# A fused two-block network on one core: modulation rows of tiles 4 to 11 formed by GpSimd instead of TensorE

## The chip, the cores and the metric

The kernel runs on one core of a Trainium2 chip (trn2). The metric is the device time of one launch in microseconds (us). Three timed runs of the kernel before gave 2313.67 us as the median, with 2313.07 and 2315.28 as the ends.

## What is computed

The input is `x`, 256 tokens of 1024 numbers, and a conditioning vector `c` of 1024. The first block begins with a modulation vector that scales, shifts and gates the later steps:

```python
mod = jax.nn.silu(c) @ w_ada[l] + b_ada[l]          # w_ada: 1024 x 6144
shift_m, scale_m, gate_m, shift_f, scale_f, gate_f = jnp.split(mod, 6, axis=-1)
h = rmsnorm(x, g_pre_mix[l]) * (1.0 + scale_m) + shift_m
...                                                 # projection, retention, dilated attention
x = x + gate_m * rmsnorm(mixed, g_post_mix[l])
h = rmsnorm(x, g_pre_ffn[l]) * (1.0 + scale_f) + shift_f
moe = expert_choice_moe(h, w_router[l], w_gate_e[l], w_up_e[l], w_down_e[l])
x = x + gate_f * rmsnorm(moe, g_post_ffn[l])
```

`mod` has 6144 numbers, which the kernel makes in twelve tiles of 512 columns. Tiles 0 to 3 give `shift_m` and `scale_m`, which the first projection needs. Tiles 4 to 11 give `gate_m`, `shift_f`, `scale_f` and `gate_f`, which are needed only after the output projection of the mixer. Sixteen experts follow, and then two layers of a second block.

## The kernel before, in words

All is in float32, and the large products of the mixer are split into a high and a low part, with three matmuls in place of one. Each engine has its own program (`@block.sync` for the loads, `gpsimd`, `tensor`, `scalar`, `vector`), and they meet only at semaphores. The order inside each program is written out by hand.

**Loads.** SyncE issues all loads in one order, `first_tiles()` (line 101): the first four modulation tiles, win 3, win 4, ada 4, ada 5, win 5, win 0, ada 6, win 1, ada 7, win 2, ada 8, wout 0, ada 9, wout 1, ada 10, ada 11, and then the tiles of the experts ("ada" is a tile of `w_ada`, "win" of the input projection, "wout" of the output projection; each has 2 MB, 4096 floats in each partition). Even ada tiles from 4 on lie in ring slot 2, odd ones in slot 3; the others alternate between slots 0 and 1. A load waits until the tile before it in its slot is used (`load`, line 571, waits for `tile_done`), and what stands behind it in the queue waits with it. So the load of ada 7 waits for the release of ada 5 and stands behind that of win 1, which waits for the release of win 5.

**A modulation tile from 4 on.** TensorE's `modulation(i)` (line 790) waits for the tile and makes eight products with `silu_c` as stationary operand, 32 equal columns of it, in four groups of 32 rows of one PSUM bank (bank 7 for all of tiles 4 to 11); each product is two matmul instructions. It then releases the slot. VectorE's `modulation(i)` (line 1840) copies the bank to `modrow[i % 2]`, 128 partitions x 512. TensorE's `modulation_columns(i)` (line 803) makes four columns of it, with `first_rows`, which is 1 in four partitions and 0 elsewhere, as the vector that sums the four groups. VectorE's `modulation_columns(i)` (line 1850) adds the bias and writes four columns of `mod`. In TensorE's list the calls stand between the units of the input projection, attention, retention and the output projection (lines 969 to 1070), in VectorE's list between its own steps (lines 1999 to 2074).

**Around it.** A projection tile goes through ScalarE (`split_first`, line 1418, casts the high part) and VectorE (`split_first`, line 1865, subtracts the high part from the raw tile in two halves of 128 x 2048, line 1869) before TensorE's `win_unit` or `wout_products` uses it. Between the tiles VectorE also makes the constants of the later layers (`layer_constants`, line 1920: seventeen instructions of 28 or 20 elements, each of which waits for the one before it), the decay arguments (lines 1943 to 1945) and the attention sums (line 1976). TensorE's last work before the normalisation of the mixer's output is `wout_products` with the first four blocks of the mixer's output (lines 1064 to 1068), behind `modulation_columns(11)`.

**GpSimd** writes constants at the start (lines 716 to 731) and then has nothing until the layers of the second block (lines 735 to 749).

## Time and profile before

| | |
|---|---|
| median of three runs | 2313.67 us |
| span of the profiled execution | 2312.3 us (the profile states no other time for it; the median is 1.4 us above the span) |
| TensorE matmul busy | 2014.7 us, 87% |
| VectorE busy | 1018.0 us, 44% |
| ScalarE busy | 727.7 us, 31% |
| GpSimd busy | 28.3 us, 1%, 23 instructions |
| DMA | 657.03 MB, mean 284 GB/s |

Times in the trace count from the start of the span. The mixer of the first block runs from about 42 to 182 us, normalisation and routing to about 228 us, the sixteen experts to about 1150 us, and the rest is the second block. "Busy" leaves out the time in which an engine waits or issues; "idle before" is the wait ahead of an instruction with what ended it.

### The profile page before, as it was taken

What the parts mean: (1) busy time and instruction counts of PE and PEld (TensorE: products, weight loads), DVE (VectorE), ACT (ScalarE), POOL (GpSimd) and SP (SyncE); (2) the same over time, 40 slices, a digit from 0 to 9 for tenths busy, and PEclk for the clock granted to TensorE, in tenths of its full rate; (3) what the DMA queues carried; (4) which work ended last, traced back from release to release, by engine and by line L of the source; (5) the groups of instructions that cost most, each with busy time, mean ns of one, the idle gap of its engine ahead of it and who ended that gap; (6) DMA issues with size and microseconds to landing.
All of it is one profiled execution on the core that took longest, in us unless ns stands there. A gap on an engine that the chain in (4) does not pass through costs nothing.

```text
span 2312.3 us, 30721 instructions
## 1 busy us (share of the span) xinstructions
PE 2014.7 (87%) x12679; PEld 1488.8 (64%) x12680; DVE 1018.0 (44%) x1136; ACT 727.7 (31%) x799; POOL 28.3 (1%) x23
## 2 busy tenths in 40 slices
PE   7997877777777777776699999999999999999999
PEld 6886333333333333333378899998888889998888
DVE  5653000000000000000277786877777767777776
ACT  3542000000000000000144446554444444745443
POOL 0000000000000000000000002000000000200000
PEclk9996978788887778887899999999999999999999
DMA  8784999999999999999935665455565566545554
GB/s 318 250 333 177 382 430 427 430 427 430 427 429 427 430 427 430 427 430 427 403 136 171 163 207 178 159 198 191 149 210 182 160 186 210 183 151 196 183 161 131
DMA packets 233161, 657.03 MB, mean 284 GB/s; under 512 B 6948, under 2 KB 121956, under 8 KB 208484
## 3 DMA queue, kind: packets, MB, share of 16 engines
q1 hardware_dynamic: 233060, 655.62, 74.1%
q8 instruction: 71, 1.16, 0.2%
q14 instruction: 30, 0.25, 0.0%
HBM read 654.54 MB, written 1.05 MB: 284 GB/s over the span
## 4 chain that ended last, share of the span: by engine, by line
issue 85%; PE 13%; DVE 1%; POOL 1%; ACT 0%; DVEq 0%; POOLq 0%; ACTq 0%
PE psum L1219 3%; PE psum L1220 2%; PE psum L1241 2%; PE psum L1242 2%; PE psum L1243 2%; PE psum L1320 2%; PE psum L1321 1%; DVE ring_r L2151 1%; PE psum L1287 0%; POOL work L742 0%; ACT ring_r L1624 0%; PE psum L1288 0%; POOL work L741 0%; POOL work L743 0%; DVE x L2447 0%
## 5 line engine op out<-in xcount | busy, mean ns | idle before, releaser
L2151 DVE TENSOR_TENSOR ring_r<-ring,ring_r 128x2048 fp32r<-128x2048 f32 (+2 forms) x182 | 452.7, 2518 | 100.7 <-ACT ring_r L1624 100.0
L1624 ACT CAST ring_r<-ring 128x2048 fp32r<-128x2048 f32 (+2 forms) x180 | 360.1, 2041 | 289.4 <-PE psum L1321 121.7
L1219 PE MATMUL psum<-work_r,ring_r 128*128 128x512 f32 x1280 | 446.3, 394 | 3.3 <-DVE ring_r L2151 3.3
L1220 PE MATMUL psum<-work_r,ring_r 128*128 128x256 f32 x1280 | 357.7, 279 | 0.0
L1219 PEld LDWEIGHTS psum<-work_r,ring_r 128*128 128x128 f32 x1280 | 239.8, 187 | 59.1 <-issue 3.9
L1136 PE MATMUL psum<-ring,work 128*32 128x512 f32 x1280 | 185.2, 716 | 101.2 <-DMA ring<-in_w_up_e_dram 101.2
L1241 PE MATMUL psum<-work_r,ring_r 128*128 128x256 f32 x928 | 263.7, 284 | 2.5 <-DVE ring_r L2151 2.5
L1242 PE MATMUL psum<-work_r,ring_r 128*128 128x256 f32 x928 | 262.4, 283 | 0.0
L1243 PE MATMUL psum<-work_r,ring_r 128*128 128x256 f32 x928 | 262.0, 282 | 0.0
L1320 PE MATMUL psum<-work_r,ring_r 128*128 128x512 f32 x704 | 247.9, 397 | 3.2 <-DVE ring_r L2151 3.2
L1220 PEld LDWEIGHTS psum<-work_r,ring_r 128*128 128x128 f32 x1280 | 241.5, 189 | 0.0
L2140 DVE COPY work<-psum 128x256 f32<-128x256 f32 x16 | 6.8, 425 | 464.8 <-PE psum L1117 464.8
L1321 PE MATMUL psum<-work_r,ring_r 128*128 128x256 f32 x704 | 197.5, 280 | 0.0
L1136 PEld LDWEIGHTS psum<-ring,work 128*32 128x32 f32 x1280 | 39.8, 121 | 237.6 <-DMA ring<-in_w_up_e_dram 154.7
L2145 DVE TENSOR_TENSOR work<-work,psum 128x512 f32<-128x512 f32 x16 | 11.0, 687 | 410.2 <-PE psum L1136 410.2
L1241 PEld LDWEIGHTS psum<-work_r,ring_r 128*128 128x128 f32 x928 | 177.2, 191 | 5.2 <-issue 4.0
L1242 PEld LDWEIGHTS psum<-work_r,ring_r 128*128 128x128 f32 x928 | 177.3, 191 | 0.1
L1243 PEld LDWEIGHTS psum<-work_r,ring_r 128*128 128x128 f32 x928 | 177.1, 191 | 0.0
L1320 PEld LDWEIGHTS psum<-work_r,ring_r 128*128 128x128 f32 x704 | 132.1, 188 | 36.0 <-issue 4.3
L2226 DVE TENSOR_REDUCE work<-psum 128x512 f32<-128x1024 f32 x88 | 107.3, 1221 | 75.5 <-PE psum L1220 68.7
L1158 PE MATMUL psum<-work 128*32 128x512 f32 x512 | 84.6, 794 | 55.9 <-DMA work<-in_w_down_e_dram 55.9
L1321 PEld LDWEIGHTS psum<-work_r,ring_r 128*128 128x128 f32 x704 | 133.0, 189 | 0.0
(301 smaller groups left out, 2388.4 us busy)
## 6 DMA issues: line engine op xcount, KB each, us to landing
ring<-in_w_up_e_dram SPq DMA_DIRECT2D x48, 2048.0 KB, 28.6
ring<-in_ffn_w_up_dram SPq DMA_DIRECT2D x41, 2048.0 KB, 8.0
work<-in_w_gate_e_dram SPq DMA_DIRECT2D x32, 2048.0 KB, 11.6
ring<-in_w_gate_e_dram SPq DMA_DIRECT2D x32, 2048.0 KB, 14.2
ring<-in_w_down_e_dram SPq DMA_DIRECT2D x32, 2048.0 KB, 36.6
work<-in_w_down_e_dram SPq DMA_DIRECT2D x32, 2048.0 KB, 30.3
ring<-in_w_in_dram SPq DMA_DIRECT2D x25, 2048.0 KB, 8.2
ring<-in_ffn_w_down_dram SPq DMA_DIRECT2D x32, 1408.0 KB, 7.0
```

What stands on the lines that cost most here:

```text
L1136: mm = pe.matmul(dst[32 * g:32 * g + 32, :], xe[:, 2 * q + k, :], w[:, k, 512 * g:512 * (g + 1)], start=(q == 0 and k == 0), stop=(q == FB ...
L1158: mm = pe.matmul(two_banks[1][32 * b:32 * b + 32, 512 * half:512 * (half + 1)], hiddenT[:, b, 32 * q:32 * q + 32], w[:, b, 512 * half:512 ...
L1219: pe.matmul(dst, w_hi[:, k, cols], h_both(k), start=(k == 0), stop=False)
L1220: mm = pe.matmul(dst[:, 0:S], w_lo[:, k, cols], h_hi_[:, S * k:S * (k + 1)], start=False, stop=(k == KD - 1))
L1241: pe.matmul(out_b, w_hi[:, k, cols], hi[:, tokens], start=(k == 0), stop=False)
L1242: pe.matmul(out_b, w_hi[:, k, cols], lo[:, tokens], start=False, stop=False)
L1243: mm = pe.matmul(out_b, w_lo[:, k, cols], hi[:, tokens], start=False, stop=(k == n_k - 1))
L1320: pe.matmul(dst, w_hi[:, k, :], u_both(k), start=(k == 0), stop=False)
L1321: mm = pe.matmul(dst[:, 0:S], w_lo[:, k, :], u_hi[:, S * k:S * (k + 1)], start=False, stop=(k == FK - 1))
L1624: act.copy(hi_unit(name, unit), raw_unit(name, unit)).then_inc(hi_ready, 1)
L2151: dve.tensor_tensor(lo_unit(name, unit), raw_unit(name, unit), hi_unit(name, unit).bitcast(F32), ALU.subtract).then_inc(lo_ready, 1)
L2226: dve.tensor_reduce(dst.rearrange("p (c t) -> p c t", c=2), src, AX.X, ALU.add).then_inc(emptied["dve"], 1)
```

## The change

GpSimd makes the rows of tiles 4 to 11. It waits for the tile, multiplies each of its eight blocks of 512 in place by its column of `silu_c` (one number in each partition), and adds the blocks as a tree: 2048 elements, then 1024, then 512 from the last two blocks into `modrow[i % 2]`. After each of the three steps and after the eighth product it waits for its own completion. The last addition waits for TensorE's columns of tile i - 2; only behind it are the slot released and the row announced. TensorE sums over all 128 partitions with a vector of ones, and its wait for VectorE's addition of the tile before (`mod_ready`) moves from the products to the columns. TensorE's products and VectorE's copies of tiles 4 to 11 go. Tiles 0 to 3 and the order of the loads stay.

```diff
@@ constants, GpSimd
             pool.memset(mean_d[:], 1.0 / D)
+            pool.memset(ones_col[:], 1.0)
@@ GpSimd, behind its constants
+            def modulation(i):
+                name = ("ada", i)
+                s = ring_plan.slot(name)
+                w = slot_view(name, KD, 512)
+                halves = w.rearrange("p k (b n) -> p k b n", b=2)
+                pool.wait_ge(loaded[s], ring_plan.loaded(name))
+                for k in range(KD):
+                    scaled = pool.tensor_scalar(w[:, k], w[:, k], silu_c[:, k, 0:1], None, ALU.mult)
+                step(scaled)
+                step(pool.tensor_tensor(w[:, 0:4], w[:, 0:4], w[:, 4:8], ALU.add))
+                step(pool.tensor_tensor(w[:, 0:2], w[:, 0:2], w[:, 2:4], ALU.add))
+                pool.wait_ge(modT_done, max(4, i - 1))
+                step(pool.tensor_tensor(modrow[i % 2], halves[:, 0], halves[:, 1], ALU.add))
+                pool.sem_inc(tile_done[s], 1)
+                pool.sem_inc(modrow_ready, 1)
+
+            pool.wait_ge(silu_c_ready, 1)
+            for i in range(4, 12):
+                modulation(i)
@@ TensorE
-            def modulation(i):
-                rows = mod_bank(i)
-                pe.wait_ge(mod_ready, i)
-                name = ("ada", i)
-                pe.wait_ge(loaded[ring_plan.slot(name)], ring_plan.loaded(name))
-                w = slot_view(name, KD, 512)
-                for k in range(KD):
-                    g = k % 4
-                    mm = pe.matmul(rows[32 * g:32 * g + 32, :], silu_c[:, k, :], w[:, k, :],
-                                   start=(k < 4), stop=(k >= KD - 4), skip_group_check=True)
-                mm.then_inc(tile_done[ring_plan.slot(name)], 1)
...
                     pe.wait_ge(modrow_ready, i if i >= 4 else {1: 1, 0: 2, 3: 3}[i])
+                if i >= 4:
+                    pe.wait_ge(mod_ready, i)
                 for c in range(4):
                     mm = pe.matmul(mod_bank(i)[:, c:c + 1], modrow[i % 2][:, c // 2, P * (c % 2):P * (c % 2 + 1)],
-                                   first_rows[:], start=True, stop=True)
+                                   (first_rows if i < 4 else ones_col)[:], start=True, stop=True)
@@ the lists of TensorE and of VectorE, eight places in each
-            modulation(4)
...
-            modulation(11)
```

## Rows read from the trace of the kernel before

**Rows 1.** Busy time in stretches: engine busy (instructions), PEclk, DMA share, GB/s

```profile
60.00:70.00 10.00, 10.00 (x85) 8.39 (x85) 3.87 (x7) 4.88 (x4) 0.00 (x0) 1.00 0.32 96
...
170.00:180.00 10.00, 10.00 (x86) 10.00 (x85) 0.44 (x4) 1.09 (x2) 0.00 (x0) 1.00 0.98 407
...
200.00:210.00 10.00, 9.62 (x45) 9.35 (x46) 3.38 (x13) 6.95 (x16) 0.00 (x0) 0.50 0.00 0
```

**Rows 2.** Groups of TensorE, 55 to 182 us: busy, mean ns, idle before

```profile
L799 PE MATMUL psum<-ring,work 128*32 128x512 f32 x128 | 15.4, 598 | 0.0
```

**Rows 3.** Timeline of TensorE: start us, us, line

```profile
60.91 1.92 PE L799 MATMUL psum<-ring,work 128*32 128x512 f32 x16
62.77 0.39 PE L904 MATMUL psum<-work_r,ring_r 128*128 128x256 f32 x1
...
72.42 0.50 PE L894 MATMUL psum<-ring_r,work_r 128*128 128x512 f32 x1
...
168.88 0.95 PE L810 MATMUL psum<-first_rows,pool_u 128*128 128x1 f32 x8
...
181.16 0.28 PE L1044 MATMUL psum<-work_r,ring_r 128*128 128x256 f32 x1
```

**Rows 4.** Timeline of GpSimd, 1398 to 1417 us

```profile
1398.86 2.00 POOL L741 TENSOR_TENSOR work<-pool_u 128x1084 f32<-128x1084 f32 x1 [1395.84 <-DVE pool_u L2214]
1400.93 3.46 POOL L742 TENSOR_TENSOR work<-work 128x807 f32<-128x807 f32 x1
1404.47 1.07 POOL L743 TENSOR_TENSOR work<-work 128x530 f32<-128x530 f32 x1
...
1410.96 5.74 POOL L749 TENSOR_TENSOR work<-work 128x2560 f32<-128x2560 f32 x1 [4.59 <-ACT work L1738]
```

**Rows 5.** Timeline of VectorE over the same stretch

```profile
1400.09 2.92 DVE L2151 TENSOR_TENSOR ring_r<-ring,ring_r 128x2048 fp32r<-128x2048 f32 x1 [1.31 <-ACT ring_r L1624]
...
1408.41 2.28 DVE L2151 TENSOR_TENSOR ring_r<-ring,ring_r 128x2048 fp32r<-128x2048 f32 x1
...
1411.21 9.84 DVE L2151 TENSOR_TENSOR ring_r<-ring,ring_r 128x2048 fp32r<-128x2048 f32 x2
```

**Rows 6.** Timeline of GpSimd at the start

```profile
1.19 0.29 POOL L717 TENSOR_SCALAR_AFFINE_SELECT ident<-ident 128x128 f32<-128x128 f32 x1 [0.24 <-POOL ident L716]
...
1.61 0.56 POOL L722 IOTA work<- 128x512 f32 x1
```

**Rows 7.** Groups of VectorE, 45 to 170 us: busy, mean ns, idle before

```profile
L1869 DVE TENSOR_TENSOR ring_r<-ring,ring_r 128x2048 fp32r<-128x2048 f32 x14 | 31.9, 2285 | 4.0 <-ACT ring_r L1425 3.9
L1976 DVE CUSTOM_DVE_ANT_0 work<-work 128x256 f32<-128x256 f32 x16 | 6.1, 419 | 0.0
L1848 DVE COPY pool_u<-psum 128x512 f32<-128x512 f32 x8 | 5.5, 690 | 12.4 <-PE psum L799 12.4
...
L1945 DVE TENSOR_TENSOR work<-work 128x512 f32<-128x512 f32 x4 | 2.8, 694 | 0.1
...
L1894 DVE TENSOR_TENSOR ring_r<-ring,ring_r 128x512 fp32r<-128x512 f32 x3 | 2.1, 685 | 0.0
L1944 DVE TENSOR_SCALAR work<-work,soft 128x512 f32<-128x512 f32 x4 | 1.9, 486 | 0.1
...
L1928 DVE SCALAR_TENSOR_TENSOR soft<-soft 128x28 f32<-128x28 f32 x8 | 1.5, 188 | 0.3
```

**Rows 8.** Timeline of SyncE's queue, 34 to 86 us: issues of loads

```profile
34.11 2.14 SPq L580 DMA_DIRECT2D ring<-in_w_ada_dram  x2
...
84.57 0.37 SPq L580 DMA_DIRECT2D ring<-in_w_in_dram  x1
84.98 0.58 SPq L580 DMA_DIRECT2D ring<-in_w_ada_dram  x1
```

**Rows 9.** Issues, KB and us to landing: tile 4's, then tile 7's

```profile
ring<-in_w_ada_dram SPq DMA_DIRECT2D x1, 2048.0 KB, 11.8
...
ring<-in_w_ada_dram SPq DMA_DIRECT2D x1, 2048.0 KB, 13.2
```

**Rows 10.** Timeline of TensorE, one matmul early and one late in the first projection

```profile
42.46 0.41 PE L871 MATMUL psum<-work_r,ring_r 128*128 128x256 f32 x1
...
48.37 0.28 PE L871 MATMUL psum<-work_r,ring_r 128*128 128x256 f32 x1
```

More of the change, by code:

```diff
@@ L318, in block_kernel @@
         mean_d = sb("mean_d", [P, 1])
+        ones_col = sb("ones_col", [P, 1])
         std = sb("std", [P, 8])
@@ L975, in _ @@
             att_scores(0)
-            modulation(5)
             win_unit(4)
@@ L981, in _ @@
             att_transpose(0)
-            modulation(6)
             win_unit(6)
@@ L993, in _ @@
             att_transpose(3)
-            modulation(7)
             win_unit(10)
@@ L1000, in _ @@
             att_transpose(5)
-            modulation(8)
             ret_scores(0)
@@ L1007, in _ @@
             ret_values(0)
-            modulation(9)
             ret_values(1)
@@ L1014, in _ @@
             att_values(3)
-            modulation(10)
             pe.wait_ge(att_done, ATT_HEADS // 2)
@@ L2000, in _ @@
             layer_constants()
-            modulation(4)
             split_first(("win", 5), (0,))
@@ L2006, in _ @@
             decay_log(0)
-            modulation(5)
             att_sums(0)
@@ L2016, in _ @@
             split_first(("win", 0), (1,))
-            modulation(6)
             decay_log(1)
@@ L2029, in _ @@
             split_first(("win", 2), (1,))
-            modulation(7)
             att_scores(6)
@@ L2039, in _ @@
             att_scores(7)
-            modulation(8)
             ret_decay(0)
@@ L2046, in _ @@
             ret_decay(2)
-            modulation(9)
             ret_decay(3)
@@ L2051, in _ @@
             split_first(("wout", 1), (1,))
-            modulation(10)
             mixin_low_att(1)
@@ L2072, in _ @@
                                   ALU.subtract).then_inc(mixin_lo_ready, 1)
-            modulation(11)
             modulation_columns(11)
```

## The prediction, made before the changed kernel was run

> **What bounds the kernel now.** I began with the busy time in stretches. Up to about 182 us TensorE is busy in the whole of every stretch, at a granted clock of 1.00, which is 2.4 GHz [rows 1]; so the mixer lasts as long as TensorE's list. At 200 us the DMA share is 0.00 [rows 1]: the first nine expert tiles are in, and nothing is loaded until the experts start at about 228 us. So whatever moves TensorE's end of the mixer, 181.4 us (the last matmul of wout starts at 181.16 [rows 3]), moves the experts and the end of the kernel by as much, and later loads cost nothing while those tiles still land before the experts start.
>
> Then the groups of the engines that the change touches. The products to be removed are 128 matmuls, 15.4 us busy with no wait ahead of them [rows 2]. The timeline shows what one tile takes of TensorE's list: from 60.91 to 62.77, 1.86 us [rows 3]; eight take 14.9 us. VectorE's copies take 5.5 us, most of the wait ahead of them being for these products [rows 7].
>
> Last the only places where GpSimd does arithmetic, in the second block, laid beside VectorE [rows 4, 5]. VectorE's subtraction of 128 x 2048, both inputs in SBUF, takes 2.28 us when GpSimd rests. Two of them issued at 1411.21 took 9.84, although they need 4.5: GpSimd had begun 2560 elements at 1410.96 and held them until 1416.70, and 1416.70 + 4.5 is about 1421.05. At 1400.09 a third took 2.92: it got going when GpSimd's 1084 elements ended at 1400.86. GpSimd's next instruction then took 3.46 for 807 elements, since VectorE held it until 1403.01. One excludes the other in both directions, and whoever waits goes next.
>
> **What is removed.** TensorE: 14.9 us of its list. VectorE: 5.5 us. Neither counts unless the columns are ready when TensorE comes to them.
>
> **What is added.** A column product against ones in place of the four-row vector has the same shape: nothing. The one memset is beside the start: nothing. What costs is GpSimd's tile, 11 instructions:
> - Additions: 2048 elements at the rate of the 2560 row (5.74) are 4.6 us; 1024 by the 1084 row (2.00) 1.9; 512 by the 530 row (1.07) 1.05 [rows 4]. Together 7.6. With the rate of the short rows for all of them it would be 3.7 + 1.9 + 0.95 = 6.5.
> - Products: no row shows a multiplication of 512 by a column. Below, the write-only iota of 512 takes 0.56 with its overhead, and a one-input select of 128 takes 0.29 [rows 6]; I take 0.43 as the lower end, the bare rate of the iota. Above, a two-input addition of 530 takes 1.07 [rows 4]. One input read and one output written is nearest to the iota: 0.6. Eight are 4.8 us.
> - So a tile is 12.4 us where TensorE needed 1.86, and eight are 99 us; their 24 waits for completion (0.07 between rows at 1404.39 and 1404.47 and the like) add 2.
>
> The Trainium skill, in "GPSIMD Engine Reference", section 3.1, gives 4497 ns for an addition of 2048 and 769 ns for a loop over 512. The first agrees with the 4.6 above; by the second the products would be 6.2 us a tile, and the end some 11 us later than mine.
>
> **The shared resource.** VectorE's instructions in this stretch that read two tensors in SBUF, or one at more than one element a cycle, are 31.9 + 6.1 + 2.8 + 2.1 us, twice 1.9 for the two kinds of scalar step ahead of line 1945, 1.5 + some 2.0 for the small ones of the constants, and about 1 for the rest [rows 7]; the scalar steps count because 0.49 us for 512 elements is under the 0.69 of the addition. About 51 us. Copies from PSUM and reductions don't count. Tile 4 lands at 34.11 + 11.8 = 45.9 [rows 8, 9]. GpSimd's last tile thus ends no earlier than 45.9 + 99 + 2 + 51 = 198 us.
>
> That this can't be beaten by order: TensorE's own wait for a VectorE result is longer too. From 46 us VectorE's steps alternate with GpSimd's. Ten or so of VectorE's until 54.6 take 7 us longer. Sixteen of the seventeen small constants each wait for one GpSimd instruction, 12.4/11 = 1.1 us on average: the chain that ended at 60.6 ends at about 81. Behind it in VectorE's list stands the subtraction of win 5, which then ends at about 86. TensorE, which began win 5 at 72.42 [rows 3], would be ready at 70.6 and waits until 86: 15 us. The release of win 5 at 84.57 goes to about 99, and with it, in SyncE's queue, the load of win 1 and behind it that of tile 7 (84.98 [rows 8]), which lands 13.2 later [rows 9], at 112. GpSimd, done with tile 6 at about 103, stands idle for 8 us, of which VectorE uses half. So 198 + 4 = 202 us for tile 11.
>
> Between 112 and 202 GpSimd goes from tile to tile in 17 to 19 us each, 12.4 of its own and 5 of VectorE's; TensorE waits for columns 10 until about 188, and then needs some 14 us to come to columns 11, at 202 too. Both ways give the same point.
>
> **The tail.** Columns 11 start at 168.88 now [rows 3] and at 202 then: 33 us later, the wout products behind them take as long. After the wait they start at the lower level of the clock: at 200 us, behind waits, the granted clock is 0.50, which is 1.2 GHz [rows 1], and a matmul early in the mixer takes 0.41 us against 0.28 for the same one later [rows 10]. I add 2 us for that, between nothing and the 4 that two cold starts would cost. The experts' loads into slots 2 and 3 wait for tiles 10 and 11, until 202; the six behind take 5.2 us each at 407 GB/s [rows 1] and are in at about 233, against a start of the experts at 263. Covered, as is the rest behind.
>
> **Sum.** 33 + 2 = 35 us on the profiled execution of 2312.3 us of span. The median stands 1.4 us above that span, and the same is added: 2312.3 + 1.4 + 35 = 2348.7, say 2348 us, 1.5% slower. A measurement of this kernel can tell about 0.2%, 4.6 us.
>
> The Trainium skill's rule that speaks against this change is in "SBUF — State Buffer", "Who interferes with whom": an exclusive lock for an instruction's whole length between GpSimd and VectorE's instructions with two SBUF inputs. Rows 4 and 5 agree, in both directions; without the lock the sum would be that of rival A.
>
> **Rivals.**
> - **A. No exclusion in this stretch** (not slower). GpSimd's tile is 12.6 us beside VectorE. The load of tile 10 stands behind that of wout 1, which waits for TensorE's last unit of win 2, now about 7 us earlier, at 124; tile 10 lands at about 140 and is ready at 152.5. TensorE comes to columns 10 at 152.4 now and gains nothing until there; it then saves the products of tile 11, 1.9 us, and a little more. 2311 us. It decides if VectorE's steps of 2.28 us stay 2.28. For it speaks only that the excluded operations in rows 5 are of one kind; against it both rows. 7%, of which 3% with cheap products as well, when it is over 4.6 us faster.
> - **B. Cheap GpSimd.** Products 0.43 and additions 6.5: 10 us a tile, 19 less in eight. 202 - 19 is 183, 15 us late, 16 to 17 with a little more idling. 2331 us. For it: the short rows at 1.9 ns an element [rows 4]. 20%.
> - **C. Dear products**, 1.07 as for two inputs [rows 4]: 30 us more over eight tiles, and about 3 more as VectorE's small steps wait longer and the load of tile 7 comes later: 2348 + 33 = 2381 us. A product of 0.8 gives some 14 us more than mine, 2362. 20% for anything above 2362.
> - **D. The small steps slip in** between GpSimd's instructions and don't wait: the chain of constants ends at 68, TensorE's 15 us go, but GpSimd's eight tiles stay, and 8 us less is all: 2340. It lies within the forecast.
>
> Forecast (with D) 53%, A 7%, B 20%, C 20%. The forecast's own range is 2336 to 2362. For 8 in 10 I leave out A, the lowest of B and the upper part of C: 2326 to 2380. Faster 0.03; same 0.04, the rest of A; slower 0.93. That GpSimd doesn't do the work is no case: TensorE's columns have no other source.
>
> **What would show it.** Right: VectorE's subtractions at line 1869 of 3 us and more on average in place of 2.28, the wait of TensorE for the first half of win 5 about 15 us, GpSimd busy or blocked almost without a gap from 46 to 202 us with 17 to 19 us a tile after tile 7, columns 11 at about 202, waits of TensorE for GpSimd at columns 10 and hardly at 4 to 7, and experts that take as long as before. Wrong: line 1869 at 2.28 (A); products of 0.45 or of 1 us (B, C); additions of 2048 at 3.7 us; TensorE's longest wait elsewhere than at win 5 and columns 10; or an expert stage that absorbs or adds time.

## The result, and the profile after

The changed kernel took 2386.97 us (median of four runs, 2385.57 to 2388.2); the kernel before, beside it, 2313.37 us (median of four, 2311.38 to 2315.28). The ratio is 1.0311, with a 95% interval of 1.0299 to 1.0323: 73.6 us slower. The forecast of 2348 us had the sign right and the size at less than half, and its range ended at 2380.

GpSimd's groups of the profile after, from 44 to 240 us (line, engine, operation, shapes, count | busy us, mean ns of one | idle time before and what ended it):

```profile
L745 POOL TENSOR_SCALAR ring<-ring,work 128x512 f32<-128x512 f32 x64 | 117.9, 1859 | 45.0 <-DMA ring<-in_w_ada_dram 43.0 <-POOL pool_u L750 2.0
L747 POOL TENSOR_TENSOR ring<-ring 128x2048 f32<-128x2048 f32 x8 | 37.6, 4701 | 0.7
L748 POOL TENSOR_TENSOR ring<-ring 128x1024 f32<-128x1024 f32 x8 | 20.9, 2613 | 0.6
L750 POOL TENSOR_TENSOR pool_u<-ring 128x512 f32<-128x512 f32 x8 | 12.3, 1533 | 0.6
```

The only wait for a load is the first, 43.0 us until tile 4 is in; behind it GpSimd works without a gap. Its timeline shows the first and the last tile; beside the last, VectorE had almost nothing to share:

```profile
46.04 15.97 POOL L745 TENSOR_SCALAR ring<-ring,work 128x512 f32<-128x512 f32 x8 [42.99 <-DMA ring<-in_w_ada_dram]
...
217.13 13.08 POOL L745 TENSOR_SCALAR ring<-ring,work 128x512 f32<-128x512 f32 x8 [0.29 <-POOL pool_u L750]
230.29 4.58 POOL L747 TENSOR_TENSOR ring<-ring 128x2048 f32<-128x2048 f32 x1
234.94 2.34 POOL L748 TENSOR_TENSOR ring<-ring 128x1024 f32<-128x1024 f32 x1
237.36 1.26 POOL L750 TENSOR_TENSOR pool_u<-ring 128x512 f32<-128x512 f32 x1
```

VectorE's only wide instructions beside it are four at 224.65 to 227.3, of which these two read two tensors in SBUF; one of the eight products, that of 226.37, took 2.30 us and the other seven 1.56:

```profile
226.02 1.29 DVE L2068 TENSOR_TENSOR work_r<-work,work_r 128x512 fp32r<-128x512 f32 x2
```

Eight products with none of that beside them take 12.35 us, as in experiment 8, so one begins every 1.54 us:

```profile
170.55 12.35 POOL L746 TENSOR_SCALAR ring<-ring,work 128x512 f32<-128x512 f32 x8 [0.29 <-POOL pool_u L751]
```

With additions of 4.49, 2.34 and 1.26 us and the steps between them a tile alone is 21.0 us, and eight are 168; the span from 46.04 to 238.62 is 192.6, so sharing with VectorE adds 25.

TensorE's waits, first in the view of waits (us in total, times, longest), then in its timeline, and the last matmul of the output projection:

```profile
PE psum L822 <- POOLq L752: 56.6, 6, 13.7
```

```profile
238.81 1.87 PE L822 MATMUL psum<-ones_col,pool_u 128*128 128x1 f32 x8 [5.57 <-POOLq L752]
...
253.73 0.28 PE L1049 MATMUL psum<-work_r,ring_r 128*128 128x256 f32 x1
```

Against [rows 3] the columns of tile 11 start 238.81 - 168.88 = 69.9 us later and the last matmul 253.73 - 181.16 = 72.6. That is the 73.6 us within 1 us. The experts behind take as long as before: VectorE's copies for the first and the last expert start 864.8 us apart (before 864.7):

```profile
L2136 DVE COPY work<-psum x16: 424/425/425, 300.4 to 1165.2; 128x256 f32<-128x256 f32 x16
```

VectorE's subtractions and attention sums, and in between the constants, from 45 to 240 us (compare [rows 7]: 2285 and 419 ns):

```profile
L1873 DVE TENSOR_TENSOR ring_r<-ring,ring_r 128x2048 fp32r<-128x2048 f32 x14 | 40.4, 2895 | 1.1 <-ACT ring_r L1429 1.1
L1980 DVE CUSTOM_DVE_ANT_0 work<-work 128x256 f32<-128x256 f32 x16 | 20.9, 1339 | 0.0
...
L1939 DVE TENSOR_SCALAR nsp<-soft 128x20 f32<-128x20 f32 x1 | 4.5, 4503 | 0.0
...
L1932 DVE SCALAR_TENSOR_TENSOR soft<-soft 128x28 f32<-128x28 f32 x8 | 2.4, 297 | 0.3
```

One instruction of 20 elements took 4.5 us: it came beside the addition of 2048. The eight at line 1932 came beside products and took 0.30 each on average, where the prediction had let each wait for 1.1. So there are two kinds of GpSimd work here, and the experiments take them apart.

### The profile page after: what moved, and what is told of

Its sections match the earlier page's. It is cut to its first block, busy times and chain, and to the rows that moved or that the text cites. A ratio compares the mean times of both kernels' runs of the same rounds, so it can differ in the third digit from the quotient of the medians.

```text
span 2385.1 us, 30565 instructions
## 1 busy us (share of the span) xinstructions
PE 2018.9 (85%) x12552; PEld 1502.0 (63%) x12552; DVE 1048.0 (44%) x1128; ACT 727.7 (31%) x799; POOL 216.9 (9%) x112
## 3 DMA queue, kind: packets, MB, share of 16 engines
HBM read 654.54 MB, written 1.05 MB: 275 GB/s over the span
## 4 chain that ended last, share of the span: by engine, by line
issue 76%; PE 13%; POOL 9%; DVE 1%; DMA 1%; SPq 0%; ACT 0%; DVEq 0%; POOLq 0%; ACTq 0%
POOL ring L745 5%; PE psum L1223 3%; PE psum L1224 2%; POOL ring L747 2%; PE psum L1245 2%; PE psum L1246 2%; PE psum L1247 2%; PE psum L1324 1%; POOL ring L748 1%; PE psum L1325 1%; DVE ring_r L2147 1%; POOL pool_u L750 1%; DMA ring<-in_w_ada_dram 0%; PE psum L1291 0%; SPq L599 0%
```

## The experiments

The theory at this point: GpSimd's pace sets the time, since it is busy without a gap and the last columns follow it; the products cost 1.5 to 1.6 us where I had 0.6; the additions keep VectorE out, the products hardly. The rivals: the time is made of VectorE's lateness; or of TensorE's lower clock behind its waits. The sum of TensorE's waits left room for the last: 56.6 us for GpSimd and 8.1 for VectorE, less 14.9 of removed products, is 50 and not 73.

**1. Prices alone.** The kernel before, with single GpSimd instructions put where GpSimd had been idle and VectorE waits.

```diff
+            pool.wait_ge(onehot_ready, 1)
+            for n in (128, 256, 512, 1024):
+                step(pool.tensor_scalar(scratch[:, 0:n], scratch[:, 0:n], col, None, ALU.mult))
+            for n in (128, 512, 1024):
+                step(pool.tensor_scalar(scratch[:, 0:n], scratch[:, 0:n], 0.5, None, ALU.mult))
+            for n in (128, 512):
+                step(pool.tensor_tensor(scratch[:, 0:n], scratch[:, 0:n], scratch[:, 512:512 + n], ALU.add))
+            for n in (128, 512, 1024):
+                step(pool.tensor_tensor(scratch[:, 0:n], scratch[:, 0:n], col.broadcast_to([P, n]), ALU.mult))
+            for n in (128, 512):
+                step(pool.tensor_copy(scratch[:, 0:n], scratch[:, 512:512 + n]))
```

> The kernel before, with GpSimd instructions on an unused buffer added at the start of the experts, where VectorE is nearly idle; each waits for the one before it. This prices the product by itself. In the changed kernel a product of 512 by a column takes 1.56 us and starts 1.63 after the one before. Theory P1, a fixed cost for the column operand: products of 128, 256, 512, 1024 take about 1.25, 1.35, 1.56, 2.0 us, and products by a constant 0.5 to 0.7 us at 512. Theory P2, a rate of 3 ns an element whatever the operand: 0.45, 0.8, 1.56, 3.1 us, and the same with a constant. Theory P3, contention with VectorE made up most of it: 0.6 us at 512 here. An addition of 512 should take 1.1 to 1.3 us, and a product of 512 by a column spread over the elements (two inputs) as much. The whole kernel: within 0.3% of before, since GpSimd has nothing else to do there.

The one run took 2311.56 us, the kernel before beside it 2314.81 (median): within the 0.3% that was expected. GpSimd's groups in it:

```profile
L740 POOL TENSOR_SCALAR pool_mix<-pool_mix,mean_d 128x1024 f32<-128x1024 f32 x1 | 2.8, 2842 | 0.1
L742 POOL TENSOR_SCALAR pool_mix<-pool_mix 128x1024 f32<-128x1024 f32 x1 | 2.8, 2769 | 0.1
L746 POOL TENSOR_TENSOR pool_mix<-pool_mix,mean_d 128x1024 f32<-128x1024 f32 x1 | 1.9, 1892 | 0.1
L740 POOL TENSOR_SCALAR pool_mix<-pool_mix,mean_d 128x512 f32<-128x512 f32 x1 | 1.6, 1564 | 0.1
...
L744 POOL TENSOR_TENSOR pool_mix<-pool_mix 128x512 f32<-128x512 f32 x1 | 1.3, 1270 | 0.1
L746 POOL TENSOR_TENSOR pool_mix<-pool_mix,mean_d 128x512 f32<-128x512 f32 x1 | 1.0, 1039 | 0.1
```

A product of 512 by a column takes 1.564 us with nobody beside it, and 2.842 at 1024: (2.842 - 1.564)/512 = 2.5 ns an element. A constant as factor costs nearly the same (2.769 at 1024), so most of it is the one-input form and not the reading of the column; that is P2 of the expectation, with a slope of 2.5 ns where it had 3. The same product written with two inputs, the second being the column spread over the row, takes 1.039 and 1.892: 1.67 ns an element. The one-input form is the dearer one, dearer even than the addition of two tensors.

**2. No products.** The eight products are left out, the additions stay.

```diff
-                for k in range(KD):
-                    scaled = pool.tensor_scalar(w[:, k], w[:, k], silu_c[:, k, 0:1], None, ALU.mult)
-                step(scaled)
```

> The changed kernel without the eight products of each tile (so tiles 4 to 11 are summed without their factors silu(c)); additions, waits and columns are unchanged. GpSimd's tile falls from 21.7 us alone to about 8.5. Theory A, the price of the products is what made the change 73 us slower, through GpSimd being late for TensorE: most of it goes, and the kernel is between 2307 us (no exclusion between VectorE and GpSimd: 6.6 us faster than before) and 2324 us (each of GpSimd's additions blocks VectorE and the other way round: 10 us slower). Theory B, the loss is mainly from waits on VectorE and the queues, whatever the products cost: more than 2340 us.

2337.94 us, ratio 1.0103 (1.0069 to 1.0138): 50 of the 73 us are gone, fewer than theory A had, and the time lies between the two theories' bands. GpSimd's and VectorE's groups:

```profile
L744 POOL TENSOR_TENSOR ring<-ring 128x2048 f32<-128x2048 f32 x8 | 43.2, 5404 | 91.4 <-DMA ring<-in_w_ada_dram 90.9 <-POOL pool_u L747 0.5
...
L1870 DVE TENSOR_TENSOR ring_r<-ring,ring_r 128x2048 fp32r<-128x2048 f32 x14 | 49.8, 3568 | 0.6 <-ACT ring_r L1426 0.6
L1977 DVE CUSTOM_DVE_ANT_0 work<-work 128x256 f32<-128x256 f32 x16 | 26.9, 1716 | 0.0
```

GpSimd now waits for loads (90.9 us) and TensorE never for GpSimd. What remains is VectorE: its subtractions take 3.57 us against 2.29, more than in the changed kernel, and TensorE's waits for VectorE and ScalarE add up to 24 us.

**3. No additions.**

```diff
-                step(pool.tensor_tensor(w[:, 0:4], w[:, 0:4], w[:, 4:8], ALU.add))
-                step(pool.tensor_tensor(w[:, 0:2], w[:, 0:2], w[:, 2:4], ALU.add))
                 pool.wait_ge(modT_done, max(4, i - 1))
-                step(pool.tensor_tensor(modrow[i % 2], halves[:, 0], halves[:, 1], ALU.add))
+                step(pool.tensor_copy(modrow[i % 2], halves[:, 0]))
```

> The changed kernel without GpSimd's additions: the eight products of a tile stay, and one copy of the first product's 512 columns goes into the modulation row in their place. It leaves out the sum over the other seven parts of the contraction in tiles 4 to 11. GpSimd takes 8 times 1.63 and about 0.6, so 13.7 us a tile. Theory A (the one-input products leave VectorE's two-input work alone; the exclusion comes from two-input instructions of GpSimd alone): VectorE's subtractions at L1873 fall from 2.90 us to their 2.3, its decay products at L1948 to under 0.8; eight tiles take 110 us, the last one is held by its load rather than by GpSimd and is done at 165 to 175, so that TensorE makes the columns of tile 11 at about the time of the kernel before (168.9); 2300 to 2316 us. Theory B (the products hold VectorE too, for a part of each): VectorE's subtractions stay at 2.6 us or more and the time is 2325 to 2345 us.

2331.53 us, ratio 1.0068 (1.0041 to 1.0095). GpSimd, VectorE, and the products' shortest, median and longest in ns:

```profile
L745 POOL TENSOR_SCALAR ring<-ring,work 128x512 f32<-128x512 f32 x64 | 119.9, 1891 | 51.8 <-DMA ring<-in_w_ada_dram 50.3 <-POOL pool_u L748 1.4
...
L1871 DVE TENSOR_TENSOR ring_r<-ring,ring_r 128x2048 fp32r<-128x2048 f32 x14 | 33.4, 2392 | 7.6 <-ACT ring_r L1427 7.5
L1978 DVE CUSTOM_DVE_ANT_0 work<-work 128x256 f32<-128x256 f32 x16 | 8.5, 569 | 0.0
```

```profile
L745 POOL TENSOR_SCALAR ring<-ring,work x64: 1557/1566/5838, 46.1 to 179.0; 128x512 f32<-128x512 f32 x64
```

58 of the 73 us are gone. VectorE's subtractions came as theory A had them, 2.39 us on average, 0.1 more than before; its time didn't, and 2331.53 lies in theory B's band. The products suffer: the median is 1.57 us, and one took 5.84, 4.27 more; VectorE's timeline has two subtractions back to back in that tile:

```profile
47.58 4.48 DVE L1871 TENSOR_TENSOR ring_r<-ring,ring_r 128x2048 fp32r<-128x2048 f32 x2
```

So VectorE's two-input work holds the products up. Whether a product holds VectorE depends on when the two meet. Here are two places of this run, each with a product, the subtraction that began beside it, and the next product:

```profile
65.28 1.57 POOL L745 TENSOR_SCALAR ring<-ring,work 128x512 f32<-128x512 f32 x1
66.38 2.29 DVE L1871 TENSOR_TENSOR ring_r<-ring,ring_r 128x2048 fp32r<-128x2048 f32 x1 [3.40 <-ACT ring_r L1427]
66.83 3.28 POOL L745 TENSOR_SCALAR ring<-ring,work 128x512 f32<-128x512 f32 x1
...
141.98 1.56 POOL L745 TENSOR_SCALAR ring<-ring,work 128x512 f32<-128x512 f32 x1
142.10 2.71 DVE L1871 TENSOR_TENSOR ring_r<-ring,ring_r 128x2048 fp32r<-128x2048 f32 x1
143.52 2.72 POOL L745 TENSOR_SCALAR ring<-ring,work 128x512 f32<-128x512 f32 x1
```

A subtraction that began 1.10 us behind the product's start took its 2.29, one that began 0.12 behind it took 0.43 more, and one at 0.34 behind (155.24, the product at 154.90) took 2.49, 0.2 more. All three fit a product that keeps VectorE out until 0.55 us after its start and has no use for the shared access after that: the products of 65.28 and 141.98 took no longer than alone, 1.57 and 1.56. That is B's mechanism, a part of each product, at 0.1 us on average where B had 0.3 or more. A product that comes to its start while VectorE has the access waits until VectorE is done, and these waits are the loss here: I had worked with 13.7 us a tile without them; products of 1.89 on average, and 7 us more of waits for loads than in the changed kernel, put the last row at 181.2 us and the last matmul at 195.6, 14.4 late.

**4. The products as one two-input instruction.**

```diff
-                for k in range(KD):
-                    scaled = pool.tensor_scalar(w[:, k], w[:, k], silu_c[:, k, 0:1], None, ALU.mult)
-                step(scaled)
+                step(pool.tensor_tensor(w, w, silu_c[:, :, 0:1].broadcast_to([P, KD, 512]), ALU.mult))
```

> The changed kernel with the eight products of a tile as one instruction: the whole tile of 4096 columns times the factors, each spread over its 512 columns (two inputs, in place). By the run with prices alone a two-input product took 1.892 us for 1024 columns (1.67 ns a column), so 4096 take about 7 us where eight one-input products take eight times 1.63, 13.1. A tile is then 7.0 + 4.5 + 2.35 + 1.26 = 15.1 us alone, not 21.7. Theory A (GpSimd's pace from 46 us to the last tile sets the time, and TensorE's columns of tile 11 follow it): eight tiles take 121 us and 20 to 35 of sharing with VectorE, or are held by their loads; the last ends at 187 to 205, TensorE makes the columns of tile 11 then, 18 to 36 us after its time in the kernel before; 2313 + 21 to 40, so 2334 to 2353 us, ratio 1.009 to 1.017. Theory B (the two-input product keeps VectorE's two-input instructions out for its whole 7 us, so that the gain of a cheaper product is paid back as waits on VectorE): GpSimd ends as early but TensorE's waits move to VectorE, 2355 to 2375 us. Theory C (the products' number or price is not what makes the change slow): 2380 us or more.

2383.47 us, ratio 1.0296 (1.0275 to 1.0318): nearly as slow as the change. It is beyond theory B's band and lies in theory C's, but the trace shows B's mechanism, larger than B had priced it. GpSimd's timeline (one product early, one later with its addition), then VectorE's over the later ones:

```profile
65.61 7.04 POOL L744 TENSOR_TENSOR ring<-ring,work 128x4096 f32<-128x4096 f32 x1 [0.26 <-POOL pool_u L748]
...
117.27 7.16 POOL L744 TENSOR_TENSOR ring<-ring,work 128x4096 f32<-128x4096 f32 x1 [13.29 <-DMA ring<-in_w_ada_dram]
124.50 4.57 POOL L745 TENSOR_TENSOR ring<-ring 128x2048 f32<-128x2048 f32 x1
```

```profile
117.56 7.15 DVE L1946 TENSOR_SCALAR work<-work,soft 128x512 f32<-128x512 f32 x1
124.74 4.87 DVE L1947 TENSOR_TENSOR work<-work 128x512 f32<-128x512 f32 x1
```

The price came as computed, 7.04 us in place of 12.35. But two steps of VectorE of 0.49 and 0.69 us alone [rows 7] took 7.15 and 4.87, from just after GpSimd's start to 0.3 and 0.5 us after the end of its instruction. TensorE waited up to 12.8 us for VectorE, the slots came free late, and GpSimd itself waited 78.8 us for loads. The same arithmetic, 43% cheaper, gained 3 us of 73, within the spread of its two runs (2379.14 and 2387.81): it had become the kind that excludes for its whole length.

**5. GpSimd's work beside the kernel before**, on scratch data of its own; nobody waits for it. Sixty-four products of 512, and three additions of 1024 and one of 512 for each tile.

```diff
+            for i in range(4, 12):
+                for k in range(KD):
+                    part = scratch[:, 512 * (k % 2):512 * (k % 2 + 1)]
+                    scaled = pool.tensor_scalar(part, part, mean_d[:, 0:1], None, ALU.mult)
...
+                for _ in range(2):
+                    step(pool.tensor_tensor(scratch, scratch, scratch, ALU.add))
+                step(pool.tensor_tensor(scratch, scratch, scratch, ALU.add))
+                step(pool.tensor_tensor(scratch[:, 0:512], scratch[:, 0:512], scratch[:, 512:1024], ALU.add))
```

> The kernel before, in which GpSimd beside it does the same instructions as in the change (eight products of 512, additions adding up to 2048, 1024 and 512 for each of eight tiles, one after the other from the landing of tile 4), but on a buffer that nobody reads; TensorE makes the rows as before and nobody waits for GpSimd. It shows contention alone. Theory C, contention for the shared SBUF access costs little of the 73 us and being late for columns the most: under 12 us slower, VectorE's 2048-wide subtractions 2.9 us on average instead of 2.28. Theory D, each product keeps VectorE out for all of its 1.56 us, so that VectorE's chains bound the mixer: over 40 us slower.

2320.12 us, ratio 1.0024 (1.0011 to 1.0038). VectorE's subtractions took 2.82 us and its sums 1.09, about as in the changed kernel, and this cost 5 us, which is theory C. So VectorE's lateness at this density is mostly hidden under TensorE's own work.

**6. One tile fewer.** Tile 4 stays on TensorE as before, GpSimd forms tiles 5 to 11.

```diff
-            for i in range(4, 12):
+            for i in range(5, 12):
                 modulation(i)
...
+            modulation(4)
             win_unit(3)
             modulation_columns(4)
```

> The changed kernel with tile 4 formed by TensorE as in the kernel before (1.9 us of it), tiles 5 to 11 by GpSimd. Theory A (GpSimd's unbroken work from 46 us to the last tile sets the time): tile 5 has landed by then, so each tile is ready one tile's time, 23.5 us, earlier, unless a load holds it; columns of tile 11 at 215 to 222; TensorE, which has 14 us of work between the columns of tiles 10 and 11, still waits for each; 2362 to 2371 us, ratio 1.021 to 1.025. Theory B (the time is made of TensorE's waits of VectorE and of its clock as much as of GpSimd's pace): 2374 to 2383 us.

2372.74 us, ratio 1.0246 (1.0219 to 1.0273), 14 us faster than the change and between the two bands. GpSimd began tile 5 at 52.10, not at 46, and waited 4.7 us for tile 6 (in all 53.8 us for loads, 10.8 more than with eight tiles); so it came to the last row at 224.07, 14.5 us earlier and not 23.5. The columns and the end moved by the same 14.5 and 14:

```profile
224.26 1.01 PE L835 MATMUL psum<-ones_col,pool_u 128*128 128x1 f32 x4 [6.01 <-POOLq L752]
```

The end follows GpSimd's last row one for one; that is theory A, with loads that I had not placed.

**7. The waits filled.** Matmuls of the identity ahead of five of the columns keep TensorE busy while it waits.

```diff
+WARM_AHEAD = {5: 45, 8: 35, 9: 55, 10: 52, 11: 22}
...
+                if i in WARM_AHEAD:
+                    pe.wait_ge(mod_ready, i)
+                    for _ in range(WARM_AHEAD[i]):
+                        pe.matmul(mod_bank(i)[:, 0:P], ident[:], ident[:], start=True, stop=True)
```

> The changed kernel with matmuls of the identity (results unused) put into five waits of TensorE for GpSimd's rows, ahead of the columns of tiles 5, 8, 9, 10 and 11: 45, 35, 55, 52 and 22 of them, about 0.21 us each at the full clock, so that each wait is nearly full and the granted clock does not fall after it. Theory A (GpSimd's pace alone sets the columns of tile 11 at 238.8 us; what TensorE loses to the lower clock ahead of that is taken out of its next wait): only the stretch behind the columns of tile 11 gains, where the last matmul of the output projection came 14.9 us after them and in the kernel before 12.3; 1 to 3 us less than the changed kernel's 2387, so 2384 to 2386. Theory B (the lower clock costs some 20 of the 73 us, as the sum of TensorE's waits, 56.6 us for GpSimd and 8.1 for VectorE less 14.9 of work removed, leaves open): 2365 to 2372 us. If the filled waits overrun, the time is above 2387 by the overrun.

2390.1 us (2388.02 to 2396.88), ratio 1.0335 (1.0318 to 1.0352): 4 us above theory A's band; it can't be told from the change, whose interval (1.0299 to 1.0323) it overlaps. Busy time in two stretches, the changed kernel's first and then this one's (PE busy, PEld, DVE, ACT, POOL, PEclk, DMA share, GB/s):

```profile
160.00:200.00 40.00, 16.85 (x72) 12.32 (x72) 18.34 (x16) 10.49 (x12) 38.94 (x19) 0.66 0.39 138
200.00:240.00 40.00, 21.15 (x146) 20.49 (x142) 6.76 (x14) 4.25 (x7) 37.85 (x20) 0.76 0.46 179
```

```profile
160.00:200.00 40.00, 31.39 (x227) 27.16 (x225) 9.76 (x10) 9.19 (x10) 38.94 (x19) 0.91 0.30 104
200.00:240.00 40.00, 35.39 (x288) 35.01 (x287) 6.46 (x16) 2.27 (x4) 36.68 (x19) 0.94 0.43 168
```

The granted clock rose from 0.66 to 0.91 and from 0.76 to 0.94, and nothing came of it: the columns of tile 11 started at 237.63 and the last matmul at 251.5, 2 us earlier in the trace, and the median isn't lower; where those 2 us went isn't settled. Theory B, 20 us for the clock, is out. A chain that waits for GpSimd again and again gives back in the next wait what it wins at the clock; the sum of the waits comes out short because the work between them took longer.

**8. Only the last two tiles.** From the kernel before: tiles 10 and 11 on GpSimd, their columns behind the output projection, where TensorE waits for the normalisation anyway.

```diff
+            for i in range(10, 12):
+                modulation(i)
...
-            modulation(10)
...
-            modulation(11)
...
             spread_columns(rstd_ready, 2, bank[5], TT, rstd_spread)
+            modulation_columns(10)
             square_sums(sq_ready, 9, 5, ms_done)
             spread_columns(rstd_ready, 3, bank[5], TT, rstd_spread)
+            modulation_columns(11)
```

> GpSimd makes the rows of tiles 10 and 11 only, which give gate_f and are not needed before the end of the experts; TensorE's columns of both move into its waits during the two normalisations at 187 and 199 us, and VectorE's additions with them. TensorE's list gets shorter by 3.7 us of products and by 1.7 us of columns. Tile 10 lands at 146 and is ready at about 170, tile 11 at about 193, before TensorE comes to the columns. Theory A (lateness is the cost, GpSimd's work is free where there is room): 3 to 5 us faster than before, 2308 to 2310. Theory D (VectorE is blocked by products): no gain or slower, since VectorE's split of wout 1 and the steps behind it fall into the same time. A third way: the expert loads into slots 2 and 3 wait for GpSimd, at 170 and 193 in place of 149 and 166, and the experts start late: 0 to 10 us slower.

2315.23 us, ratio 1.0002 (0.9988 to 1.0017). GpSimd's timeline with the additions of tile 11, and VectorE's eight additions to the stream in the view of their line (shortest, median and longest in ns):

```profile
182.98 4.49 POOL L748 TENSOR_TENSOR ring<-ring 128x2048 f32<-128x2048 f32 x1
187.55 2.40 POOL L749 TENSOR_TENSOR ring<-ring 128x1024 f32<-128x1024 f32 x1
```

```profile
L2112 DVE SCALAR_TENSOR_TENSOR x<-work,gains,x x8: 472/482/4761, 183.0 to 194.4; 128x256 f32<-128x256 f32 x8
```

One addition of 0.48 us took 4.76, the length of GpSimd's. TensorE's wait there became 8.2 us, where the kernel before has 3.4, and ate what the removed products had won.

**9. The last two with the two-input product.** The diff of experiment 4 on top.

> As in the run with only tiles 10 and 11 on GpSimd, but each with one two-input product of 4096 columns. There tile 11 was done at 191.3 and its additions of 183.0 to 190 kept VectorE's additions to the stream out, for which ScalarE and then TensorE waited 8.2 us; that took the 3 to 4 us that TensorE had gained. A tile is now 15 to 16 us alone, not 21.7: tile 10 from 147 to about 163, tile 11 to about 179, before VectorE's additions begin at 182. Theory A: the wait of 8.2 us shrinks to the kernel before's 3 to 5, and the kernel is 3 to 5 us faster than before: 2308 to 2311 us, ratio 0.998 to 0.9988. Theory B (the product of 7 us, now with two inputs, keeps VectorE's work at 147 to 155 and 163 to 170 out, which is on TensorE's path there): 2314 to 2322 us.

2321.11 us, ratio 1.0029 (1.002 to 1.0039): slower, theory B. The wait of 8.2 us did shrink, to 1.9. But TensorE waited 4.9 us at 151.6 and 5.6 us at 159.4 for VectorE, inside the stretch of the product and the additions.

**10. Only tile 10.** As experiment 8, with tile 11 on TensorE.

> Only tile 10 on GpSimd, with the change's eight products and three additions; tile 11 by TensorE as in the kernel before, and both tiles' columns behind the output projection. TensorE loses 1.86 us of work for tile 10. Tile 10 is formed from 147 to about 170, under the value products and the first part of the output projection, and nobody waits for GpSimd before the columns at 182. Theory A (a tile off TensorE is worth its 1.9 us where no wait takes it back): 2311 to 2312 us, ratio 0.999 to 0.9995. Theory B (VectorE's constants are late by the two additions of 4.5 and 2.4 us between 160 and 170): 2314 to 2318 us.

2313.26 us, ratio 0.9997 (0.9988 to 1.0006). The median lies between the two theories' bands. The first expert's copy came at 224.7 us against 227.8, 3.1 us earlier, and the last at 1089.4 against 1092.5; the medians differ by 0.9. The two kernels can't be told apart, and where the rest went isn't settled.

**11. Tile 11's additions held back.** As experiment 8, but they wait until VectorE has made its eight, and the columns come behind the router.

```diff
                 step(scaled)
+                if i == 11:
+                    pool.wait_ge(x_ready, 4 + KD)
                 step(pool.tensor_tensor(w[:, 0:4], w[:, 0:4], w[:, 4:8], ALU.add))
...
             tokens_out(0)
+            modulation_columns(11)
```

> Only tiles 10 and 11 on GpSimd, as in the first such run, but tile 11's additions wait until VectorE has made the stream's eight additions (at about 194 us), and TensorE makes the columns of tile 11 after the router and the first tokens, in a wait of its own. Theory A (the additions at 183 to 190 alone took the gain of that run back): TensorE's wait for the stream falls from 8.2 us to 2 to 4, the experts start 3 to 4 us earlier than in the kernel before, 2309 to 2312 us, ratio 0.998 to 0.999. Theory B (what is gained ahead of the experts is given back behind them, as the run with tile 10 alone hints: its first expert came 3.1 us earlier and its time fell by 0.9): 2312 to 2316 us. Theory C (the additions, now at 195 to 204, hold VectorE's products for the router, or the ring slot comes free too late for an expert's weights): 2316 us or more.

> The same kernel as the run with tile 11's additions held back, timed again on its own account: there its ratio was 0.9986 with an interval of 0.9972 to 1.0, which just touches no change. Theory A (additions placed beside no two-input work of VectorE let the removed TensorE work come through): 0.998 to 0.9992, 2310 to 2313 us. Theory B (what is gained ahead of the experts is given back behind them): 0.9995 to 1.001.

2312.7 us, ratio 0.9986 (0.9972 to 1.0), and again 2313.06, 0.9991 (0.998 to 1.0002). The additions now lie in a stretch without two-input work of VectorE, and all eight of its additions are short (the first repetition's timeline of GpSimd, and the view of VectorE's line):

```profile
187.95 4.52 POOL L750 TENSOR_TENSOR ring<-ring 128x2048 f32<-128x2048 f32 x1 [6.73 <-DVE x L2114]
```

```profile
L2114 DVE SCALAR_TENSOR_TENSOR x<-work,gains,x x8: 479/480/485, 183.3 to 187.3; 128x256 f32<-128x256 f32 x8
```

TensorE's wait fell to 1.85 us, and the first expert's copy came at 223.9 us, 3.9 earlier, as theory A had it. Both ratios lie in theory A's bands, both medians 0.1 to 0.7 us above them, and each interval touches 1. Two to three us faster than the kernel before is the best reading, not one that either run shows by itself.

**12. Tile 9 as well.**

```diff
-            for i in range(10, 12):
+            for i in range(9, 12):
                 modulation(i)
...
-            modulation(9)
...
-            modulation_columns(9)
...
             group_variances()
+            modulation_columns(9)
```

> As the run with tile 11's additions held back, and tile 9 on GpSimd too, its columns made behind the group variances at about 153 us. Tile 9's load is issued at 118 us and lands at about 131; 13.1 us of products and 8.3 of additions and steps end at about 152.5. Its additions of 4.5 and 2.4 us fall on 144 to 152, where VectorE makes three subtractions of 2.3 us for the output projection, which TensorE needs at about 150. Theory A (the additions are late there by their own length): TensorE waits 3 to 6 us at 150 to 156, which is more than the 1.9 of tile 9's removal: 2313 to 2318 us. Theory B (TensorE's work between hides that too): 2308 to 2311 us.

2319.35 us, ratio 1.0021 (1.0011 to 1.0032): slower, 1 us above theory A's band. GpSimd and VectorE meet again in their timelines:

```profile
143.89 5.81 POOL L750 TENSOR_TENSOR ring<-ring 128x2048 f32<-128x2048 f32 x1
149.77 4.27 POOL L751 TENSOR_TENSOR ring<-ring 128x1024 f32<-128x1024 f32 x1
```

```profile
142.99 8.85 DVE L1896 TENSOR_TENSOR ring_r<-ring,ring_r 128x2048 fp32r<-128x2048 f32 x2 [0.50 <-ACT ring_r L1452]
```

Busy time from 155 to 165 us, here and then in experiment 11 (PE busy, PEld, DVE, ACT, POOL, PEclk, DMA share, GB/s):

```profile
155.00:165.00 10.00, 9.41 (x53) 9.41 (x54) 4.38 (x10) 1.08 (x2) 9.71 (x8) 0.62 0.88 326
```

```profile
155.00:165.00 10.00, 10.00 (x86) 10.00 (x85) 3.58 (x6) 1.22 (x2) 9.84 (x6) 1.00 0.46 195
```

Two subtractions of 2.28 took 8.85 together, the additions 5.81 and 4.27 for 4.5 and 2.35: each stood in the other's way. TensorE waited 4.5 us at 151 for GpSimd's row of tile 9 and had a granted clock of 0.62 in the stretch from 155 to 165. The first expert's copy came 7.9 us after that of experiment 11 (231.8 and 223.9), of which the wait is 4.5. I put the rest down to the clock, which no later wait takes back here; no run sets it apart.

## Why the prediction was wrong in size

**What bounds the kernel: right.** TensorE's list up to 182 us set the end, and the delay of its last matmul, 72.6 us, is the whole difference. The experts absorbed and added nothing.

**The products: the step that failed.** I took 0.6 us, between 0.43 and 1.07, "nearest to the iota"; the traces have one every 1.54 us with nothing beside it, and the run of prices has 1.564 for one alone. The upper end, a two-input addition of 530 elements, was no upper end, since the one-input form is the slower one. This term alone: (1.54 - 0.6) x 64 = 60 us. What shows it is the price (experiments 1 and 8), with experiment 6 for the end that follows GpSimd's last row one for one. Experiments 2 and 3 don't divide the 73 us: 50 came back without the products and 58 without the additions, together more than the whole, since each leaves another bound behind. No run has products of 0.6 us, so what the forecast's own price would have given was not measured.

**The additions: nearly right.** 4.58, 2.34 and 1.26 against 4.6, 1.9 and 1.05, together 8.2 and not 7.6, 4 to 5 us over eight tiles. The sentence on the Trainium skill's 4497 ns in "GPSIMD Engine Reference", section 3.1, agrees with 4.49 in experiment 8. Its 769 ns for a loop over 512, which I had set beside my own price, would have been 6.2 us a tile where 12.35 were measured, so it doesn't carry over to this product either.

**The shared resource: right in kind, much too large.** I added all of VectorE's two-input time, 51 us, to GpSimd's; it was 25. A product leaves VectorE free from 0.55 us after its start (experiment 3), so much of VectorE's work fits beside it. "Whoever waits goes next" failed too: the product of 5.84 us waited through two of VectorE's subtractions. The Trainium skill, in "SBUF — State Buffer", "Who interferes with whom", has an exclusive lock on the ports that the two engines share; its sentence on a lock for the whole instruction stands with VectorE's 2-port modes, and of VectorE's instructions with two SBUF inputs it says that they contend. A lock for the whole length agrees for GpSimd's two-input instructions (4.76 us for one of 0.48; 7.15 for one of 0.49) and for VectorE's against the products (5.84 for 1.57); it doesn't for GpSimd's products against VectorE, which were in the way for 0.55 us of their 1.56.

**The 15 us at win 5, and tile 7's late load: wrong.** I had let each of sixteen small constants (there are eighteen, not seventeen) wait for 1.1 us of GpSimd. They ran beside products, at 0.30 us, and only one met an addition. The constants ended at about 67 instead of 81, TensorE waited 0.7 us for win 5, no load was late. That was rival D, which I had priced at 8 us less. TensorE's waits came instead at the columns of tiles 4 and 5 (5.4 and 10.7 us) and 8 to 11, which I had excluded for 4 to 7.

**The tail: right.** 2 us for the clock; 72.6 - 69.9 = 2.7 in the trace, of which 1 went when experiment 7 raised the clock.

**The sum.** Predicted for GpSimd: 46 + 99 + 2 + 51 + 4 = 202. Measured: 46 + 168 + 25 = 239. The difference is 60 for products and about 6 for additions and steps, less 26 for sharing and 4 for the idle time: 36, of the 37. Two errors of opposite sign made the forecast look closer than its terms were, and that was luck.

**The rivals.** C, dear products, was the one that happened, with its price at 1.07 where it is 1.54, so that even its 2381 was short. A and B are out: VectorE's subtractions rose to 2.90, and nothing on GpSimd was cheaper than I took it by more than 0.1 us.

## What to carry to other kernels

Before work is moved to an idle engine, measure the very form of the instruction on it, alone and in the size that is meant: here the form with fewer inputs was the slower one by half, and 64 times an error of 0.94 us was the largest error of the forecast. Then ask which of its instructions exclude a neighbour's, and for how much of their length, since a cheaper form that excludes throughout can cost as much as a dear one that does so only at its start. What little there was to win here (1.9 us of TensorE a tile) came through only where the excluding instructions were put beside none of the neighbour's, and nobody waited for the slow engine.

## What the runs showed of the hardware that I had not expected

- GpSimd's product of a tensor by a column or a constant takes 2.5 ns an element (1.564 us for 512, 2.842 for 1024, float32). With the column as a spread second tensor it takes 1.67 ns (1.039, 1.892, and 7.04 us for 4096), and the addition of 512 takes 1.270.
- For the one-input product the exclusion is lopsided: VectorE's two-input instructions hold it until they are done (5.84 us beside two of them), it holds VectorE's until 0.55 us after its own start (2.71 us for one that came at 0.12, 2.29 for one that came at 1.10; 2.39 on average, against 2.29 before). GpSimd's two-input instructions hold VectorE's for their whole length, a scalar step of 512 elements and one of 20 elements among them (7.15 and 4.50 us).
- Without products, the additions alone made VectorE's subtractions longer (3.57 us) than products and additions together (2.90). The additions then come right behind each load, where VectorE has its subtractions to do; I think that is why, but no run here sets it apart.
